# Two experts per pass of the expert loop, their rows gathered together

## The reference, cut to what matters

```python
logits = (xt @ w_router)
top_logit, top_idx = lax.top_k(logits, 2)          # 8 experts, 2 per token
gates = jax.nn.softmax(top_logit, axis=-1)
# rows of each expert gathered, padded to blocks of 128
ys = (silu(xs @ w_gate[e]) * (xs @ w_up[e])) @ w_down[e]    # 1024 -> 3584 -> 1024
out = zeros.at[token].add(ys * gate)
```

## Time and profile before

| what | value |
|---|---|
| median of three runs | 1790.84 us |
| the profiled execution | 1788.93 us |
| its span, first to last instruction | 1787.1 us |
| PE busy | 1735.0 us (97%), 8636 matmuls |
| DVE busy, ACT busy | 1332.4 us (75%), 1164.3 us (65%) |
| mean TensorE clock granted | 0.99 |
| read from HBM | 477.51 MB |
| instruction queues q8 and q14 | 0.61 MB and 0.16 MB |

### The profile page before, as it was taken

One profiled execution on the slowest core, in us unless ns is written; L12 is line 12 of the kernel. 1 busy time (PEld: TensorE's weight loads), 2 busy tenths in 40 slices (PEclk: granted clock), 3 DMA queues, 4 the chain that ended last, 5 costly groups with the idle time before them and its releaser, 6 DMA issues.

```text
span 1787.1 us, 23458 instructions
## 1 busy us (share of the span) xinstructions
PE 1735.0 (97%) x8636; PEld 1423.5 (80%) x8636; DVE 1332.4 (75%) x1183; ACT 1164.3 (65%) x1197; POOL 71.9 (4%) x78
## 2 busy tenths in 40 slices
PE   7999999899999999889999999999999999999998
PEld 6778888787788876678888888888888888888886
DVE  5754444675555467568888898898888888988988
ACT  5555454665444468657777677777777777777775
POOL 2200000320100010100000000000000000000000
PEclk9999999999999999989999999999999999999999
DMA  9455552644655453339999999999999999999995
GB/s 360 143 189 178 178 186 78 213 150 158 213 168 189 141 194 108 107 142 357 373 334 364 346 349 369 344 347 371 326 366 374 318 369 371 322 372 346 349 369 218
DMA packets 229041, 480.18 MB, mean 269 GB/s; under 512 B 11164, under 2 KB 54528, under 8 KB 228984
## 3 DMA queue, kind: packets, MB, share of 16 engines
q1 hardware_dynamic: 221376, 471.45, 74.2%
q10 hardware_dynamic: 7096, 7.42, 1.3%
q0 software_dynamic: 512, 0.54, 0.1%
HBM read 477.51 MB, written 1.08 MB: 268 GB/s over the span
## 4 chain that ended last, share of the span: by engine, by line
PE 70%; ACT 4%; DVE 4%; issue 2%; DMA 1%; POOL 1%; ACTq 0%; DVEq 0%; POOLq 0%
PE bank L674 21%; PE bank L677 21%; PE bank L675 21%; PE bank L1240 2%; PE bank L1127 2%; ACT w_hi L1812 1%; PE bank L1272 1%; DVE x L2370 1%; DVE w_lo L2390 1%; PE bank L668 1%; DMA decay<-decay_dram 1%; POOL decay L630 1%; ACT L1812 1%; DVE w_lo L1869 0%; ACT w_hi L1342 0%
## 5 line engine op out<-in xcount | busy, mean ns | idle before, releaser
L2390 DVE TENSOR_TENSOR w_lo<-raw,w_hi 128x2048 fp32r<-128x2048 f32 x336 | 764.5, 2290 | 118.1 <-ACT w_hi L1812 115.3
L1812 ACT ACTIVATE w_hi<-raw 128x2048 fp32r<-128x2048 f32 x336 | 639.2, 1919 | 173.1 <-PE bank L677 173.1
L1869 DVE TENSOR_TENSOR w_lo<-raw,w_hi 128x2048 fp32r<-128x2048 f32 (+3 forms) x117 | 253.0, 2167 | 146.4 <-ACT w_hi L1342 146.1
L674 PE MATMUL bank<-w_hi,xg_hi 128*128 128x512 f32 x896 | 355.3, 397 | 5.8 <-DVE w_lo L2390 4.3
L677 PE MATMUL bank<-w_hi,xg_lo 128*128 128x512 f32 x896 | 350.3, 391 | 0.0
L675 PE MATMUL bank<-w_lo,xg_hi 128*128 128x512 f32 x896 | 349.8, 390 | 0.0
L674 PE MATMUL bank<-w_hi,a_hi 128*128 128x512 f32 (+3 forms) x672 | 261.2, 389 | 11.6 <-DVE w_lo L1869 5.1
L1342 ACT ACTIVATE w_hi<-raw 128x2048 fp32r<-128x2048 f32 (+3 forms) x117 | 211.0, 1810 | 88.3 <-PE bank L677 85.3
L677 PE MATMUL bank<-w_hi,a_lo 128*128 128x512 f32 (+3 forms) x672 | 254.2, 378 | 0.0
L675 PE MATMUL bank<-w_lo,a_hi 128*128 128x512 f32 (+3 forms) x672 | 254.1, 378 | 0.0
L674 PEld LDWEIGHTS bank<-w_hi,xg_hi 128*128 128x128 f32 x896 | 168.9, 188 | 42.4 <-DVE w_lo L2390 7.3
(11 more groups left out here) (251 smaller groups left out, 1714.1 us busy)
## 6 DMA issues: line engine op xcount, KB each, us to landing
raw<-in_moe_w_gate SPq DMA_DIRECT2D x114, 1024.0 KB, 6.9
raw<-in_moe_w_up SPq DMA_DIRECT2D x113, 1024.0 KB, 7.2
raw<-in_moe_w_down SPq DMA_DIRECT2D x112, 1024.0 KB, 6.4
raw<-in_w_mlp SPq DMA_DIRECT2D x32, 1024.0 KB, 5.2
raw<-in_ffn_w_gate SPq DMA_DIRECT2D x22, 512.0 KB, 3.8
raw<-in_ffn_w_up SPq DMA_DIRECT2D x22, 512.0 KB, 4.8
raw<-in_ffn_w_down SPq DMA_DIRECT2D x11, 1024.0 KB, 4.9
raw<-in_w_in SPq DMA_DIRECT2D x9, 1024.0 KB, 11.9
```

The lines of the kernel that those rows point to most:

```text
L674: pe.matmul(o, hi, h, start=start, stop=False)
L1812: act.activation(w_hi[:, g % NSPLIT, :], raw_at(g, GRAN), ACT.Copy).then_inc(hi_made, 1)
L1869: dve.tensor_tensor(w_lo[:, g % NSPLIT, 0:n], raw_at(g, n), w_hi[:, g % NSPLIT, 0:n].bitcast(F32), ALU.subtract).then_inc(lo_made, 1)
L2390: dve.tensor_tensor(w_lo[:, g % NSPLIT, :], raw_at(g, GRAN), w_hi[:, g % NSPLIT, :].bitcast(F32), ALU.subtract).then_inc(lo_made, 1)
```

## The change

The loop's body now holds two items, u = 0 and u = 1, and runs `n_pairs` = 4 times (8 if an expert is too full). There are two sets of gathered rows, `xg_hi0`/`xg_lo0` and `xg_hi1`/`xg_lo1`. `pick` holds two experts side by side (256 columns), and one gather of 32 matmuls of 256 columns fills both sets. It is cut into four steps of 8 matmuls, each a full bank, and stands in item u = 1 alone: steps 0 and 1 behind the up granules of chunk 6, step 2 behind the first down granule, step 3 behind the second. ACT and DVE take each bank in two instructions of 128x256, one for each set. In item u = 0 nothing stands between the up granules of chunk 6 and `chunk_t(7)`. `mf_sb`, `mf_hi` and `mf_lo` alternate by (c + u), as seven chunks is odd. Two small padding tiles keep other tiles where they were.

```diff
-MOE_TSTEPS = 3 + MOE_CHUNKS
+PAIR_TSTEPS = 2 * (MOE_CHUNKS + 1) + 4
...
-        pick = sb("pick", [P, NB, P], F32R, stack=moes)
+        sb("pad_pick", [P, NB, P], stack=moes)
...
+        pick = sb("pick", [P, NB, 2, P], F32R, stack=moes)
+        xg_hi1 = sb("xg_hi1", [P, KT, P], F32R, stack=moes)
+        xg_lo1 = sb("xg_lo1", [P, KT, P], F32R, stack=moes)
...
             def gather(k, dst):
 
-                for kk in range(4):
-                    kt = 4 * k + kk
+                for kk in range(2):
+                    kt = 2 * k + kk
                     for b in range(NB):
                         for part in (z_hi, z_lo):
-                            mm = pe.matmul(dst[:, kk * P:(kk + 1) * P], part[:, b, kt * P:(kt + 1) * P], pick[:, b, :],
-                                           start=b == 0 and part is z_hi, stop=b == NB - 1 and part is z_lo)
+                            mm = pe.matmul(dst[:, kk * S:(kk + 1) * S], part[:, b, kt * P:(kt + 1) * P], pick[:, b, :, :],
+                                           start=kk == 0 and b == 0 and part is z_hi, stop=kk == 1 and b == NB - 1 and part is z_lo)
                 mm.then_inc(t_psum, 1)
...
-                    if c == GATHER_CHUNK:
-                        pe.wait_ge(pick_made, i + 2)
-                        for kk in range(2):
-                            t_free(GATHER_STEP + kk)
-                            gather(kk, bank[6 + (TM + GATHER_STEP + kk) % 2])
+                    gathers = u == 1 and c == GATHER_CHUNK
+                    if gathers:
+                        pe.wait_ge(pick_made, pair + 2)
+                        gather_t(0)
+                        gather_t(1)
+                    elif c == GATHER_CHUNK:
                         chunk_t(c + 1)
                     if c >= 1:
-                        pe.wait_ge(t_dve, i * MOE_TSTEPS + (TD + 2 + CHUNK_STEP[c] + 1))
+                        t_made(chunk_step(u, c) + 1)
                         for half in range(2):
-                            w_ready(k)
-                            down(NG + k, lambda p, kt, b: (mf_hi, mf_lo)[p][:, (c - 1) % 2, kt, :], 2 * half,
+                            if gathers and half == 1:
+                                gather_t(2)
+                                chunk_t(c + 1)
+                            pe.wait_ge(lo_made, granules(k + 1))
+                            down(NG + k, lambda p, kt, b: (mf_hi, mf_lo)[p][:, (c - 1 + u) % 2, kt, :], 2 * half,
                                  [[bank[0][:], bank[1][:]]], c == 1 and half == 0, c == MOE_CHUNKS and half == 1)
                             k += 1
+                    if gathers:
+                        gather_t(3)
+
+            pe.wait_ge(items_made, 1)
+            pairs = pe.value_load(n_pairs[0:1, 0:1], min_val=N_EXPERTS // 2, max_val=N_EXPERTS)
+            with pe.Fori(0, pairs) as i:
+                for u in range(2):
+                    item(i, u)
...
             def xg_hi_out(k, src):
-                act.activation(xg_hi[:, 4 * k:4 * k + 4, :], src[:].rearrange("p (k s) -> p k s", k=4), ACT.Copy)\
-                    .then_inc(t_act, 1)
+                for u in range(2):
+                    ins = act.activation(xg_hi[u][:, 2 * k:2 * k + 2, :],
+                                         src[:].rearrange("p (k u s) -> p k u s", k=2, u=2)[:, :, u, :], ACT.Copy)
+                ins.then_inc(t_act, 1)
...
                     if c == GATHER_CHUNK:
                         while k <= moe_first(c) + 5:
                             e_hi(k)
                             k += 1
-                        for kk in range(2):
-                            step_in(GATHER_STEP + kk)
-                            xg_hi_out(kk, bank[6 + (TM + GATHER_STEP + kk) % 2])
+                        gathers = u == 1
+                        if gathers:
+                            gather_hi(0)
+                            gather_hi(1)
+                            e_hi(k)
+                            k += 1
+                            gather_hi(2)
                         chunk_hi(c + 1)
+                    if c == GATHER_CHUNK + 1 and gathers:
+                        gather_hi(3)
```

More of the change, by code:

```diff
@@ L1253, in _, with item, t_made, t_bank_moe @@
             pe.wait_ge(pick_made, 1)
-            for k in range(2):
+            for k in range(4):
                 pe.wait_ge(t_dve, TD + k - 1)
                 gather(k, bank[6 + (TM + k) % 2])
[L1257 to L1265, removed]
+            def item(pair, u):
+                def t_made(n):
+                    pe.wait_ge(t_dve, pair * PAIR_TSTEPS + (TD + 4 + n))
+                def t_bank_moe(n):
+                    return bank[6 + (TM + n) % 2]
+                def granules(k):
+                    return pair * (2 * MOE_GRANULES) + (u * MOE_GRANULES + NG + k)
                 def chunk_t(c):
-                    pe.wait_ge(h_made, i * MOE_CHUNKS + (HM + c))
-                    t_free(CHUNK_STEP[c])
+                    pe.wait_ge(h_made, pair * (2 * MOE_CHUNKS) + (u * MOE_CHUNKS + HM + c))
+                    step = chunk_step(u, c)
+                    t_made(step - 1)
                     for kt in range(4):
-                        mm = pe.transpose(bank[6 + (TM + CHUNK_STEP[c]) % 2][:, kt * P:(kt + 1) * P],
-                                          mf_sb[:, (c - 1) % 2, 1, kt * P:(kt + 1) * P], ident[:])
+                        mm = pe.transpose(t_bank_moe(step)[:, kt * P:(kt + 1) * P],
+                                          mf_sb[:, (c - 1 + u) % 2, 1, kt * P:(kt + 1) * P], ident[:])
                     mm.then_inc(t_psum, 1)
-                pe.wait_ge(t_dve, i * MOE_TSTEPS + (TD + 2))
+                def gather_t(n):
+                    t_made(GATHER_STEP[n] - 1)
+                    gather(n, t_bank_moe(GATHER_STEP[n]))
+                k = 0
+                if u == 0:
+                    t_made(0)
                 for c in range(MOE_CHUNKS + 1):
@@ L1828, in _ @@
                     if c == PICKG_CHUNK:
-                        step_in(PICKG_STEP)
-                        act.activation(slot_gates[:], bank[6 + (TM + PICKG_STEP) % 2][:, 0:S], ACT.Copy, accum_out=slot_gate[:])\
+                        step_in(pickg_step(u))
+                        act.activation(slot_gates[:], t_src(pickg_step(u))[:, 0:S], ACT.Copy, accum_out=slot_gate[:])\
                             .then_inc(t_act, 1)
@@ L2429, in _ @@
                         ub = bank[5] if c % 2 == 0 else bank[3]
[L2430 to L2432 removed]
+                        dve.wait_ge(silu_made, pair * (2 * MOE_CHUNKS) + (u * MOE_CHUNKS + SM + c + 1))
+                        dve.wait_ge(w_used, pair * (2 * MOE_GRANULES) + (u * MOE_GRANULES + NG + moe_first(c) + 4))
+                        dve.tensor_tensor(mf_sb[:, (c + u) % 2, 1, :], mf_sb[:, (c + u) % 2, 0, :], ub[:], ALU.mult)\
+                            .then_inc(h_made, 1)
                     if c == GATHER_CHUNK:
[L2434 to L2436 removed]
+                        if gathers:
+                            gather_lo(0)
+                            gather_lo(1)
+                            e_lo(k)
+                            k += 1
+                            gather_lo(2)
                         chunk_lo(c + 1)
+                    if c == GATHER_CHUNK + 1 and gathers:
+                        gather_lo(3)
                 for k in range(AHEAD):
                     if k == AHEAD - 1:
[L2441 removed]
+                        dve.wait_ge(y_act, pair * 2 + (u + 2))
                         y_out()
                     e_lo(MOE_GRANULES + k)
+            dve.wait_ge(items_made, 2)
+            pairs = dve.value_load(n_pairs[0:1, 0:1], min_val=N_EXPERTS // 2, max_val=N_EXPERTS)
+            with dve.Fori(0, pairs) as i:
+                for u in range(2):
+                    item(i, u)
             for n in range(4):
[L2445 removed]
+                dve.wait_ge(sc_psum, pairs * 8 + (n + 1))
                 add_y(n)
```

150 lines of the change are left out of this document (84 added, 66 removed).

## The result

The changed kernel takes 1793.63 us (median of 20 runs, 1788.92 to 1796.4); the kernel before, run on the same chip beside it, 1790.9 us (20 runs). The ratio is 1.0014, with a 95% interval of 1.0009 to 1.002: slower by 0.14%, a little, but more than the measurement's uncertainty. I had forecast 1788.8 us. The time lies in the predicted range, on the other side of the kernel before.

The account below looks back on a forecast made before the run. PE's own row of work was taken to bound the expert loop. Four pairs -4.1, first gather -1.3 and clock falls +3.4 summed to -2.0 us, for a median of 1788.8 us, range 1783.5 to 1794.7 us.

Parts of the forecast that it names:

- Between pairs it stays.: Jump from one pair to the next: PE's wait of 0.62 us for DVE's split remains as before.
- Rival 4: Full DVE or larger loop adds small waits in u = 1, up to 1 us per pair: 1792.8 us, chance 0.08.
- the product's wait: Chunk 7's transposes in u = 0: PE waits 2.79 us for DVE's product, +2.91 us per pair with the slower restart.
- the range's upper end: 1794.7 us: clock falls in all four waits and the first gather does not raise it.
- first gather: Ahead of the loop: between +1.2 us and, if it raises the clock, -2.6 us; -1.3 us taken.
- The merged gather: Item u = 1: 32 matmuls of 256 columns at 0.120 us take 3.84 us instead of 3.52, +0.32 us per pair.
- The boundary inside a pair: Between u = 0 and u = 1: no table load, so the 0.62 us wait and its restart go, -0.74 us.
- The clock fell three times rather than two: Behind the four waits at the transposes: two falls taken at 1.7 us each, +3.4 us.
- Rival 1: Clock stays up in all four waits at the transposes: 1785.4 us, chance 0.17.
- Rival 2: Clock falls in every wait and the first gather doesn't raise it: slower, 1794.7 us with four falls, chance 0.16.
- Rival 3: Product ready in time at u = 0's transposes, wait hidden: 15.8 us gained in four pairs, 1773.7 us, chance 0.04.
- 81 ns for a stream: Skill page's price for a 128-column matmul streamed with weight loads; the prediction used the trace's 0.110 us instead.

Follow-up runs that it names:

- last experiment: Kernel before with its eight items written one behind the other, no jump back in the loop, gathers of 128 columns kept: 1784.56 us, ratio 0.9967.
- the filled wait: Changed kernel with 11 thrown-away matmuls of 512 columns on PE ahead of chunk 7's transposes in u = 0: 1789.85 us, ratio 1.0.
- the later transposes: Changed kernel with chunk 7's transposes in u = 0 moved behind the first down granule and one more granule's split: 1778.39 us, ratio 0.9932.

## Why the prediction was wrong, point by point

**The step that failed** is in the part on the boundary: "Between pairs it stays." It did not stay. It became 2.33, 2.15 and 1.97 us of waits in place of 0.62 us. With their restarts (PE's steps of 0.95 + 1.70, 0.73 + 1.74 and 0.55 + 1.74 us beyond the usual one, against 0.78 us, and one more restart of 0.11 us) that is 7.41 - 2.34 + 0.33 = +5.4 us where the sum had nothing. Read from the distances between the four waits at L1291 it is the same: 251.60, 251.60 and 249.86 us from one pair to the next, where the prediction had 250.1 us with a fall of the clock and 248.4 us without. Each is 1.5 us above, and the third has no fall. I moved instructions and counted them, but never asked what their number does to the code; the rows of q8 and q14 stood on the page of the kernel before. Rival 4 named "the larger loop" and a full DVE, at most 1 us per pair, 4 us in all, with a chance of 0.08. Its 1792.8 us lies nearest to the result, but partly by luck: it wanted the product's wait not to be the price, and the waits inside u = 1 where there are none, and for the larger loop it gave no mechanism. That the time lies in my range is luck too, as the range's upper end stood for four falls and a slow first gather.

**What held.** The product's wait: 2.63 us in the row and 2.79 us in PE's steps, four times, as forecast. The merged gather: the first matmuls of its first two steps, eight matmuls apart in the timeline, are 0.96 us apart, 0.120 us each:

```profile
1012.84 0.28 PE L1253 MATMUL bank<-pick,z_hi 128*128 128x256 f32 x1
...
1013.80 0.28 PE L1253 MATMUL bank<-pick,z_hi 128*128 128x256 f32 x1
```

The boundary inside a pair has no wait of PE, and none stands at the gather in u = 1: PE's waits in the loop are the ten of the two lines above.

**What was mis-sized.** The boundary inside a pair gives 0.95 us rather than 0.74 (last experiment), so four pairs give about -5.0 instead of -4.1 us. The first gather went to the best end of its bounds, -2.6 us, where I took -1.3 us: it did raise the clock, which was open. The clock fell three times rather than two, at 1.5 us each: +4.5 instead of +3.4 us.

**The sum with the measured terms**, for the loop: -5.0 - 2.6 + 4.5 + 5.4 = +2.3 us; its length grew by 2.65 us, and the medians by 2.7 us. Without the step that failed it would be about -3 us, near the forecast. The profiled executions differ by 5.45 us, but 2.86 us of it lie ahead of everything that the change touches: the router's first matmul starts at 757.43 instead of 754.57. That belongs to the one execution of the kernel before, not to the kernel: in its variants with one body doubled or without a jump that matmul starts at 756.39 to 757.16.

**The clock** decided nothing alone. Rival 1, no falls, was met by the filled wait (1789.85 us against its 1785.4): still no gain, since the jumps take it. Rival 2 had the right side for the wrong reason: the first gather did raise the clock, and three falls cost less than the jumps (4.5 against 5.4 us). Rival 3, the product in time, has its gain in the later transposes: 12.1 us under the kernel before instead of 17, the rest lost at the jumps.

The Trainium skill, page "TensorE: Matmul & The Clock Gate", section "Back-to-back issue gap", has 262 cycles (109 ns) as the isolated gap of one matmul of 256 columns. The measured step is 0.120 us in the loop, as in the earlier trace rows: a tenth more. It is a figure of another kind than the 81 ns for a stream that the prediction set beside it.

## What to carry to other kernels

Unrolling a hardware loop is a change of its own: look first whether an instruction queue moves anything inside the loop. If none does, the body is kept, and a longer one can bring a reload behind every jump. Taking a jump away gave 1.7 to 3.3 us here, of which some 0.95 us is what a boundary of the short body costs too. Stay under that size, or leave the jump out altogether. And work that covers a hand-over of a product is not free to take away: the merged gather paid only once another granule, ready by then, stood in its place.

## What the runs showed of the hardware

- A loop's body above some length is loaded again in every pass, 5 packets for DVE and 11 or 12 for PE here. How long a body may be was not tried: DVE's and PE's body of one item is kept, that of two items is not; ACT's body of two items shows no idle time behind the jump, that of four items 2.3 to 2.4 us.
- The first instruction behind the jump starts at a fixed distance behind such a packet: DVE's split 1.9 us behind one of q14 at all six jumps of the changed kernel and of the kernel with DVE's body doubled, PE's matmul 2.6 to 2.7 us behind one of q8 at all three jumps with PE's body doubled. In the changed kernel DVE's start is 2.1 us later than ACT's copy would let it. Why the packet itself comes only 3.2 us after DVE's sequencer has reached the head of the loop (1031.54 to 1034.76) was not tried; in that stretch q1 with its weights fills the DMA engines' time (102.7% in the view).
- The same code costs no idle time of DVE when it is read straight on, though as many packets bring it.
- The clock's answer to the same gap of 2.63 us differed within one execution: three falls and one stay, in the changed kernel behind the first, second and fourth wait, with two pairs per pass behind the second, third and fourth.
- The first gather of 128 columns stayed at the lower clock throughout, in all five profiled kernels that have it. With 256 columns the clock rose 3.3 us into it here, and in all six kernels that have it before the loop began, once only after 6.1 us (two pairs per pass).
- DVE's and PE's reloads cost 4.4 us and 1.9 us alone, in three jumps each. With all three bodies doubled the kernel is 3.7 us slower, where the two less 3.8 us for its inner boundaries would give 2.5 us (by the loop's length 3.0 against 3.7 us). No run shows that one reload hides the other.
